# Low parts of weights made by GpSimd in the first mixer, and its chunks placed on consecutive groups

## The chip, the cores and the metric

The kernel runs on one core of one Trainium2 chip. The metric is device time in microseconds of the whole kernel, lower is better. Times come from repeated runs and from one execution that the hardware profiler recorded. Engines are named as in the profile: PE (TensorE), DVE (VectorE), ACT (ScalarE), POOL (GpSimd), SP (SyncE, which here only issues transfers).

## The reference

Two layers of a decoder trunk on x of 256 tokens by 2048 features, all in float32. Each layer has a mixer and an MLP, both modulated by a condition vector c:

```python
cond = silu(c)
for l in range(2):
    sh1, sc1, g1, sh2, sc2, g2 = split(cond @ w_mod[l] + b_mod[l], 6)      # w_mod[l]: 2048 x 12288
    u = x * (1 + sc1) + sh1
    q, k, v, gate_b, gate_c, h_in = split(u @ w_in[l])                     # w_in[l]: 2048 x 6144
    attn = dilated_mixture(rotary(q), rotary(k), v)                        # 8 heads of 128
    conv = gate_b * causal_short_conv(gate_c * h_in, conv_w[l])
    mixed = group_rms_norm(concat(attn, conv), mix_norm_g[l])
    x = layer_norm(alpha * x + (1 + g1) * (mixed @ w_out[l]), ...)         # w_out[l]: 2048 x 2048
    u = x * (1 + sc2) + sh2
    ff = square(relu(u @ w_ff1[l])) @ w_ff2[l]                             # 2048 x 8192, 8192 x 2048
    x = layer_norm(alpha * x + (1 + g2) * ff, ...)
```

## The kernel before, in words

**Units, groups, labels.** Every large product is cut into units of 512 output columns, and a unit into 8 groups (`GROUPS`) of two 128-row blocks of the weights. One group of weights is 128 partitions by 1024 elements (`GW`), 512 KB. A label numbers the groups through the whole kernel: label = 8 * unit + j. The first mixer has 16 units (12 of `w_in`, 4 of `w_out`), labels 0 to 127. The first three units (labels 0 to 23, `START_GROUPS`) are done in another way, at the start, while the modulation for them is computed. The MLP of the layer follows with 64 units, then the second layer.

**High and low parts.** To keep float32 accuracy, weights and activations are split in a high part, as PE reads it, and the remainder, the low part. For each label from 24 on:
- SP loads the weights into `raw[:, j % 4]` (four slots, line 426). It waits until the low part of the label four before has been made, since that is the last reader of the slot.
- ACT copies them to `w_hi[:, j % 4]` (line 516, semaphore `hi_ready`). It waits for the transfer and for PE to have done the group four before.
- DVE subtracts, `w_lo = raw - w_hi` (line 836, semaphore `lo_ready`, counted in order of labels).
- PE waits for `lo_ready` and does 12 matmuls of 512 columns: for two row blocks and two token tiles, high by high, low by high, high by low (lines 1367 to 1369; in halves of one token tile lines 1381 to 1383).

ACT and DVE run `ahead`: at position p (the turn of label p) they prepare label p + 4, then do what `side` asks for at p.

**The last unit.** In the last unit of a mixer or MLP, groups 4 to 7 are done for the first token tile and then again for the second. DVE's `last_tile` (from line 1012) finishes the first tile, gives it its normalisation while PE does the second tile, and the fill of the next unit (transposes of the normalised x, line 1513) starts from there. GpSimd normalises two of the four quarters of each tile (line 483, a tensor-scalar on 128 x 512), DVE one (line 969), ACT one.

**Chunks.** The modulation is a product of c with `w_mod`, too long and thin for PE; DVE does it beside the rest, one chunk of 128 x 1024 elements (512 KB) at a time: line 858 for slabs used as columns (a multiplication by `cond_row` with a sum), lines 846 and 850 for slabs used as gates. 16 chunks make a slab. GpSimd's loop issues the chunk transfers (line 496) into four slots of `mod_raw`; each waits until DVE has done the chunk four before (`mod_used`). The list `MOD_AT`, from `mod_positions`, says at which positions DVE does a chunk: in the first mixer 96 chunks (6 slabs), at every position from 25 to 71, and from 72 to 126 at all but those with p % 8 = 7. `side` of DVE does the chunk first and then whatever else stands at p. At p % 8 = 7 of units 12 to 14 that is `residual`, which waits for the unit's last group. After the last slab that `modulation` of the next fill needs, its columns are summed.

**Order.** Each engine runs its own list, in order, and waits on counting semaphores. GpSimd's list is: chunk issues in a hardware loop of four per turn, `normalise` at each fill, and again.

Of the kernel before, what the change touches and what calls it, by code (L numbers as in the profile page):

```python
# [28 lines left out]
F32 = mybir.dt.float32  # L29
# [49 lines left out]
def mod_positions():  # L79

    mixer0 = [p for p in range(START_GROUPS + 1, 8 * U_MIX) if p % 8 != 7 or p < 72]
    ff0 = sorted([8 * w + j for w in range(2, FF_UNITS - 1) for j in (1, 3, 4, 6)]
                 + [8 * w + 7 for w in (2, 3, 8, 9, 10, 11, 16, 17, 18, 19, 24, 25)])
    mixer1 = sorted([8 * u + j for u in range(2, 15) for j in (0, 2, 4, 6)]
                    + [8 * u + 1 for u in range(2, 14)])
    ff1 = sorted([8 * w + 4 for w in range(3, 25)] + [8 * w + 1 for w in range(3, 13)])
    out = []
    for base, count, local in ((MIXER_AT[0], MIX_SLABS[0], mixer0), (FF_AT[0], FF_SLABS[0], ff0),
                               (MIXER_AT[1], MIX_SLABS[1], mixer1), (FF_AT[1], FF_SLABS[1], ff1)):
        assert len(local) == count * KC  # L90
        out += [base + p for p in local]
    return out
# [67 lines left out]
MIX_GAIN_AT = (9, 11, 13, 17)  # L160
FF_GAIN_AT = (8 + 1, 8 + 4, 8 + 6, 16 + 1)


# [43 lines left out]
def build(nc, x, cond_c, ln_cols, w_in, w_out, w_ff1, w_ff2, w_mod, b_mod, b_rows, conv_w, mix_g, ln1_g, ln1_b,  # L207
# [3 lines left out]
    with ctx:  # L211
# [90 lines left out]
        hi_ready = sem("hi_ready")  # L302
        lo_ready = sem("lo_ready")
        pair_used = sem("pair_used")
        mod_used = sem("mod_used")
# [81 lines left out]
        def prepared(unit, j):  # L387

            return 8 * unit + (j + 1 - START_GROUPS)

        def wait_job(eng, n):

# [3 lines left out]
        def _(sp):  # L396
# [22 lines left out]
            def load(weights, row, unit, j, from_head=False):  # L419
                slot = j % RAW  # L420
                if from_head and j < START_LABELS:
                    sp.wait_ge(pair_used, START_GROUPS - 2 * START_LABELS + j + 1)
                elif not from_head or j >= RAW:

                    sp.wait_ge(lo_ready, prepared(unit, j - RAW))
                sp.dma_start(raw[:, slot:slot + 1, :],
                             weights[bass.ds(row, 1), :, :].rearrange("a p n -> p a n")).then_inc(raw_in[slot], 16)

            for layer in range(DEPTH):
                base = U_LAYER * layer  # L430
                if layer == 0:
# [6 lines left out]
                    for j in range(GROUPS):  # L438
                        load(w_in, START_GROUPS + j, START_UNITS, j, from_head=True)
                first = START_UNITS + 1 if layer == 0 else 0  # L440
                with sp.Fori(first, U_IN) as u:
                    for j in range(GROUPS):
                        load(w_in, (u + layer * U_IN) * GROUPS + j, u + base, j)
                with sp.Fori(0, U_OUT) as u:
                    for j in range(GROUPS):
                        load(w_out, (u + layer * U_OUT) * GROUPS + j, u + (base + U_IN), j)
                with sp.Fori(0, BLOCKS) as b:
# [13 lines left out]
        def _(pool):  # L461
# [23 lines left out]

            ends, q = [], 0
            for count in (MIX_SLABS[0], FF_SLABS[0], MIX_SLABS[1]):
                q += count * KC
                ends.append(q // MODS + 1)
            ends.append((SLABS - START_SLABS) * KC // MODS)  # L490
            start = 1
            for i, end in enumerate(ends):
                with pool.Fori(start, end) as r:
                    for k in range(MODS):
                        pool.wait_ge(mod_used, MODS * r + (first + k - MODS + 1))
                        pool.dma_start(mod_raw[:, k:k + 1, :], chunk(r * MODS + (first + k))).then_inc(mod_in[k], 16)  # L496
                if i < 3:
                    normalise(i + 1)
# [326 lines left out]
        def _(dve):  # L825
# [7 lines left out]

            def prepare(unit, j):
                dve.wait_ge(hi_ready, prepared(unit, j))
                nc.vector.tensor_tensor(weights(w_lo, u_lo, unit, j), raw[:, j % RAW, :],  # L836
# [512 lines left out]
        def _(pe):  # L1349
# [6 lines left out]
            def group(label, slot, k0, acc_pair, hi, lo):  # L1356


                pe.wait_ge(lo_ready, label + 1 - START_GROUPS)
                for kk in range(GK):  # L1360
# [11 lines left out]
            def half(unit, j, o, t, hi, lo):  # L1372


                pe.wait_ge(lo_ready, prepared(unit, j))
                for kk in range(GK):
# [348 lines left out]
```

## Time and profile before

| what | value |
|---|---|
| runs | 2330.39, 2333.58, 7494.66 us; median 2333.58 |
| profiled execution | 2329.62 us |
| its span | 2327.9 us |
| TensorE busy | 2253.6 us (97%) |
| DVE busy | 1707.9 us (73%) |
| ACT busy | 1079.8 us (46%) |
| GpSimd busy | 227.6 us (10%) |
| mean granted TensorE clock | 0.989 of 2.4 GHz |
| transfers | 623.10 MB, 268 GB/s over the span |

The span is the time between the first and the last instruction in the profile; the execution's own time is a little longer. Busy times are sums of instruction durations, and issuing a transfer counts as GpSimd's only where a row shows it. "Landing" is the time from the issue of a transfer until its data are there. Matmuls overlap: one is shown as 0.39 us, but the next starts 0.23 us after it.

### The profile page before, as it was taken

To read this page: it belongs to the slowest core of one execution; us is meant where nothing else is said; L and a number is where in the kernel's file an instruction comes from. 1 tells how busy PE (TensorE), PEld (TensorE's weight loads), DVE (VectorE), ACT (ScalarE), POOL (GpSimd) and SP (SyncE) were. 2 spreads that over 40 slices of the span, in tenths; PEclk is the share of its full clock that TensorE was granted. 3 is DMA by queue.
4 is the path that set the end of the run, shared out by engine and by line. 5 is a ranking of instruction groups with operands and counts; after the bars stand their busy time and mean duration, and the time that the engine had idled before them with its cause. 6 is when DMAs were issued, how large, how long until landed. Compare 5 with 4: busy or idle time off the path is not lost.

```text
span 2327.9 us, 29649 instructions
## 1 busy us (share of the span) xinstructions
PE 2253.6 (97%) x10064; PEld 1824.3 (78%) x10064; DVE 1707.9 (73%) x2200; ACT 1079.8 (46%) x1372; POOL 227.6 (10%) x400
## 2 busy tenths in 40 slices
PE   6899999989999999999999999999999999999997
PEld 3368887768888888888878888877888888888886
DVE  5799988977777777778878878877665555555566
ACT  1146543366345445445454564436644543543542
POOL 2301111111001011011010111101000000000000
PEclk8999999989999999999999999999999999999999
DMA  9988998958888888888866788886677676666574
GB/s 378 409 328 303 337 343 296 362 189 277 280 293 303 277 300 302 289 293 289 315 216 219 259 271 287 297 303 204 194 235 248 223 227 217 210 203 197 173 228 134
DMA packets 174731, 623.10 MB, mean 268 GB/s; under 512 B 19728, under 2 KB 20496, under 8 KB 174096
## 3 DMA queue, kind: packets, MB, share of 16 engines
q1 hardware_dynamic: 114128, 407.50, 50.8%
q0 software_dynamic: 55296, 201.35, 25.5%
q10 hardware_dynamic: 5184, 12.59, 1.7%
q8 instruction: 80, 1.31, 0.2%
q14 instruction: 43, 0.35, 0.0%
HBM read 619.27 MB, written 2.10 MB: 267 GB/s over the span
## 4 chain that ended last, share of the span: by engine, by line
PE 84%; DVE 7%; DMA 6%; issue 2%; ACT 1%; ACTq 1%; POOLq 0%; DVEq 0%; SPq 0%; POOL 0%
PE bank L1367 26%; PE bank L1369 26%; PE bank L1368 26%; DMA Z<-w_mod_dram 4%; PE bank L1460 2%; DVE w_lo L836 2%; DMA raw<-w_out_dram 1%; DVE mod_raw L858 1%; PE bank L1381 1%; PE bank L1383 1%; PE bank L1382 1%; DVE Z L858 1%; ACT w_hi L516 1%; ACTq L588 1%; PE bank L1446 1%
## 5 line engine op out<-in xcount | busy, mean ns | idle before, releaser
L836 DVE TENSOR_TENSOR w_lo<-raw,w_hi 128x1024 fp32r<-128x1024 f32 x740 | 903.4, 1224 | 517.4 <-ACT w_hi L516 515.5
L516 ACT ACTIVATE w_hi<-raw 128x1024 fp32r<-128x1024 f32 x740 | 782.1, 1059 | 1020.5 <-PE bank L1369 915.1
L1367 PE MATMUL bank<-w_hi,u_hi 128*128 128x512 f32 x1648 | 652.8, 396 | 0.0
L1369 PE MATMUL bank<-w_lo,u_hi 128*128 128x512 f32 x1648 | 642.1, 390 | 0.0
L1368 PE MATMUL bank<-w_hi,u_lo 128*128 128x512 f32 x1648 | 641.8, 389 | 0.0
L1367 PE MATMUL bank<-w_hi,m_hi 128*128 128x512 f32 x1200 | 470.1, 392 | 4.4 <-DVE m_lo L906 2.5
L1369 PE MATMUL bank<-w_lo,m_hi 128*128 128x512 f32 x1200 | 467.8, 390 | 0.0
L1368 PE MATMUL bank<-w_hi,m_lo 128*128 128x512 f32 x1200 | 467.6, 390 | 0.0
L1369 PEld LDWEIGHTS bank<-w_lo,u_hi 128*128 128x128 f32 x1648 | 309.3, 188 | 65.3
L1367 PEld LDWEIGHTS bank<-w_hi,u_hi 128*128 128x128 f32 x1648 | 309.5, 188 | 63.9 <-issue 1.2
L1368 PEld LDWEIGHTS bank<-w_hi,u_lo 128*128 128x128 f32 x1648 | 309.7, 188 | 63.5 <-issue 1.2
L496 POOL DMA_DIRECT2D mod_raw<-w_mod_dram x316 | 167.3, 529 | 1709.3 <-DVE mod_raw L858 756.7
L1367 PEld LDWEIGHTS bank<-w_hi,m_hi 128*128 128x128 f32 x1200 | 225.7, 188 | 52.9 <-DVE m_lo L906 3.3
L1368 PEld LDWEIGHTS bank<-w_hi,m_lo 128*128 128x128 f32 x1200 | 225.7, 188 | 47.0 <-issue 0.5
L1369 PEld LDWEIGHTS bank<-w_lo,m_hi 128*128 128x128 f32 x1200 | 225.5, 188 | 47.1
L858 DVE SCALAR_TENSOR_TENSOR mod_raw<-mod_raw,cond_row 128x1024 f32<-128x1024 f32 x192 | 234.0, 1219 | 4.1 <-DMA mod_raw<-w_mod_dram 4.0
L850 DVE SCALAR_TENSOR_TENSOR mod_acc<-mod_raw,cond,mod_acc 128x1024 f32<-128x1024 f32 x120 | 153.5, 1279 | 0.0
L858 DVE SCALAR_TENSOR_TENSOR Z<-Z,cond_row 128x1024 f32<-128x1024 f32 x64 | 77.3, 1223 | 34.4 <-DMA Z<-w_mod_dram 31.0
L1497 PE MATMUL bank<-raw,utmp 128*128 128x512 f32 x96 | 48.5, 657 | 19.4 <-DMA raw<-w_in_dram 11.0
L906 DVE TENSOR_TENSOR m_lo<-utmp,m_hi 128x512 fp32r<-128x512 f32 x72 | 49.2, 692 | 13.0 <-ACT m_hi L540 12.9
L1460 PE MATMUL bank<-idn,Z 128*128 128x128 f32 x416 | 54.1, 273 | 2.5 <-DVE Z L1207 1.4
L1460 PEld LDWEIGHTS bank<-idn,Z 128*128 128x128 f32 x416 | 48.4, 141 | 9.6 <-DVE Z L1207 1.8
(151 smaller groups left out, 1257.2 us busy)
## 6 DMA issues: line engine op xcount, KB each, us to landing
raw<-w_ff_dram SPq DMA_DIRECT2D x512, 512.0 KB, 4.0
mod_raw<-w_mod_dram POOLq DMA_DIRECT2D x320, 512.0 KB, 5.2
raw<-w_in_dram SPq DMA_DIRECT2D x180, 512.0 KB, 5.3
Z<-w_mod_dram POOLq DMA_DIRECT2D x64, 512.0 KB, 12.5
raw<-w_out_dram SPq DMA_DIRECT2D x64, 512.0 KB, 5.9
gate<-w_in_dram SPq DMA_DIRECT2D x8, 512.0 KB, 8.9
gate<-b_rows_dram ACTq DMA_DIRECT2D x4, 1024.0 KB, 4.9
Z<-ln_g_dram ACTq DMA_DIRECT2D x16, 256.0 KB, 6.3
```

Of the source, the lines that this page charges most:

```text
L496: pool.dma_start(mod_raw[:, k:k + 1, :], chunk(r * MODS + (first + k))).then_inc(mod_in[k], 16)
L516: nc.scalar.activation(weights(w_hi, u_hi, unit, j), raw[:, j % RAW, :], ACT.Copy).then_inc(hi_ready, 1)
L588: act.dma_start(lngb[:, s, a, :], src[layer:layer + 1, s * NCOL:(s + 1) * NCOL] .to_broadcast([P, NCOL])).then_inc(gb_in[s], 16)
L836: nc.vector.tensor_tensor(weights(w_lo, u_lo, unit, j), raw[:, j % RAW, :], weights(w_hi, u_hi, unit, j).bitcast(F32), ALU.subtract).then_ ...
L850: ins = nc.vector.scalar_tensor_tensor(out=mod_acc[:], in0=src, scalar=cond[:, k:k + 1], in1=mod_acc[:], op0=ALU.mult, op1=ALU.add)
L858: nc.vector.scalar_tensor_tensor(out=src, in0=src, scalar=1.0, in1=cond_row[:, half], op0=ALU.mult, op1=ALU.mult, accum_out=mod_part[:, i: ...
L906: nc.vector.tensor_tensor(lo[:, chunk:chunk + 2, :], src, hi[:, chunk:chunk + 2, :].bitcast(F32), ALU.subtract).then_inc(split_ready, 1)
L1367: nc.tensor.matmul(o, hi[:, k, tok], wh, start=(k == 0), stop=False)
L1368: nc.tensor.matmul(o, lo[:, k, tok], wh, start=False, stop=False)
L1369: ins = nc.tensor.matmul(o, hi[:, k, tok], wl, start=False, stop=(k == KC - 1))
L1460: ins = nc.tensor.transpose(b[:, c * SEQ + t * P:c * SEQ + (t + 1) * P], src(c, t), idn[:])
L1497: ins = nc.tensor.matmul(start_acc[unit][t][:], utmp[:, e % 2, tok], place[:, c * NCOL:(c + 1) * NCOL], start=(s == 0), stop=(s == KC - 1))
```

## The change

It has two parts, both in the first mixer alone.

1. The 96 chunks are done at positions 24 to 119, one at each. The last unit (positions 120 to 127) has none.
2. For labels 31, 35, ..., 119 (23 of them, all in slot 3) GpSimd makes the low part. The instruction stands in GpSimd's loop behind the four chunk issues of a turn and waits for the high part of label 4r + 27. DVE skips these labels. Whoever waited for the low part of a label (PE, and SP for the raw slot) now waits for `pool_lo` on these labels, and on the others for `lo_ready` with the count reduced by GpSimd's. So that the counts are constants, SP's two hardware loops over the units of the first mixer are written out.

The start of GpSimd's loops moves by one turn for the first stage's end, so that turn r always meets label 4r + 27.

```diff
--- before.py
+++ after.py
@@ -78,7 +78,7 @@
 
 def mod_positions():
 
-    mixer0 = [p for p in range(START_GROUPS + 1, 8 * U_MIX) if p % 8 != 7 or p < 72]
+    mixer0 = list(range(START_GROUPS, START_GROUPS + MIX_SLABS[0] * KC))
     ff0 = sorted([8 * w + j for w in range(2, FF_UNITS - 1) for j in (1, 3, 4, 6)]
                  + [8 * w + 7 for w in (2, 3, 8, 9, 10, 11, 16, 17, 18, 19, 24, 25)])
     mixer1 = sorted([8 * u + j for u in range(2, 15) for j in (0, 2, 4, 6)]
@@ -159,6 +159,19 @@
 GAIN_ORDER = {1: (0, 1, 2, 3), 2: (2, 0, 1, 3), 3: (0, 1, 2, 3)}
 MIX_GAIN_AT = (9, 11, 13, 17)
 FF_GAIN_AT = (8 + 1, 8 + 4, 8 + 6, 16 + 1)
+
+
+POOL_FIRST, POOL_LAST = START_GROUPS + 2 * AHEAD - 1, START_GROUPS + MIX_SLABS[0] * KC - 1
+
+
+def on_pool(label):
+
+    return label % AHEAD == AHEAD - 1 and POOL_FIRST <= label <= POOL_LAST
+
+
+def pool_count(label):
+
+    return max(0, (min(label, POOL_LAST) - POOL_FIRST) // AHEAD + 1)
 
 def start_order(p):
@@ -301,6 +314,7 @@
         gb_in = [sem(f"gb_in{j}") for j in range(4)]
         hi_ready = sem("hi_ready")
         lo_ready = sem("lo_ready")
+        pool_lo = sem("pool_lo")
         pair_used = sem("pair_used")
         mod_used = sem("mod_used")
         cond_exp = sem("cond_exp")
@@ -388,6 +402,13 @@
 
             return 8 * unit + (j + 1 - START_GROUPS)
 
+        def wait_low(eng, label):
+
+            if on_pool(label):
+                eng.wait_ge(pool_lo, pool_count(label))
+            else:
+                eng.wait_ge(lo_ready, label + 1 - START_GROUPS - pool_count(label))
+
         def wait_job(eng, n):
 
             eng.wait_ge(t_done, n + 1)
@@ -420,9 +441,12 @@
                 slot = j % RAW
                 if from_head and j < START_LABELS:
                     sp.wait_ge(pair_used, START_GROUPS - 2 * START_LABELS + j + 1)
-                elif not from_head or j >= RAW:
-
-                    sp.wait_ge(lo_ready, prepared(unit, j - RAW))
+                elif isinstance(unit, int):
+                    if not from_head or j >= RAW:
+                        wait_low(sp, GROUPS * unit + j - RAW)
+                else:
+
+                    sp.wait_ge(lo_ready, prepared(unit, j - RAW) - pool_count(POOL_LAST))
                 sp.dma_start(raw[:, slot:slot + 1, :],
                              weights[bass.ds(row, 1), :, :].rearrange("a p n -> p a n")).then_inc(raw_in[slot], 16)
 
@@ -437,13 +461,19 @@
                     sp.wait_ge(mod_used, START_SLABS * KC - 4)
                     for j in range(GROUPS):
                         load(w_in, START_GROUPS + j, START_UNITS, j, from_head=True)
-                first = START_UNITS + 1 if layer == 0 else 0
-                with sp.Fori(first, U_IN) as u:
-                    for j in range(GROUPS):
-                        load(w_in, (u + layer * U_IN) * GROUPS + j, u + base, j)
-                with sp.Fori(0, U_OUT) as u:
-                    for j in range(GROUPS):
-                        load(w_out, (u + layer * U_OUT) * GROUPS + j, u + (base + U_IN), j)
+                    for u in range(START_UNITS + 1, U_MIX):
+                        for j in range(GROUPS):
+                            if u < U_IN:
+                                load(w_in, u * GROUPS + j, u, j)
+                            else:
+                                load(w_out, (u - U_IN) * GROUPS + j, u, j)
+                else:
+                    with sp.Fori(0, U_IN) as u:
+                        for j in range(GROUPS):
+                            load(w_in, (u + layer * U_IN) * GROUPS + j, u + base, j)
+                    with sp.Fori(0, U_OUT) as u:
+                        for j in range(GROUPS):
+                            load(w_out, (u + layer * U_OUT) * GROUPS + j, u + (base + U_IN), j)
                 with sp.Fori(0, BLOCKS) as b:
                     for half, weights in enumerate((w_ff1, w_ff2)):
                         for u in range(4):
@@ -484,9 +514,10 @@
                                                 ALU.add).then_inc(xhat_pool, 1)
 
             ends, q = [], 0
+            assert START_GROUPS + AHEAD * (MIX_SLABS[0] * KC // MODS) - 1 == POOL_LAST
             for count in (MIX_SLABS[0], FF_SLABS[0], MIX_SLABS[1]):
                 q += count * KC
-                ends.append(q // MODS + 1)
+                ends.append(q // MODS + (1 if ends else 0))
             ends.append((SLABS - START_SLABS) * KC // MODS)
             start = 1
             for i, end in enumerate(ends):
@@ -494,6 +525,11 @@
                     for k in range(MODS):
                         pool.wait_ge(mod_used, MODS * r + (first + k - MODS + 1))
                         pool.dma_start(mod_raw[:, k:k + 1, :], chunk(r * MODS + (first + k))).then_inc(mod_in[k], 16)
+                    if i == 0:
+
+                        pool.wait_ge(hi_ready, AHEAD * r + AHEAD)
+                        nc.gpsimd.tensor_tensor(w_lo[:, AHEAD - 1, :], raw[:, RAW - 1, :], w_hi[:, AHEAD - 1, :].bitcast(F32),
+                                                ALU.subtract).then_inc(pool_lo, 1)
                 if i < 3:
                     normalise(i + 1)
                 start = end
@@ -832,6 +868,8 @@
                 dve.wait_ge(dve_step, step[0])
 
             def prepare(unit, j):
+                if on_pool(GROUPS * unit + j):
+                    return
                 dve.wait_ge(hi_ready, prepared(unit, j))
                 nc.vector.tensor_tensor(weights(w_lo, u_lo, unit, j), raw[:, j % RAW, :],
                                         weights(w_hi, u_hi, unit, j).bitcast(F32), ALU.subtract).then_inc(lo_ready, 1)
@@ -1356,7 +1394,7 @@
             def group(label, slot, k0, acc_pair, hi, lo):
 
-                pe.wait_ge(lo_ready, label + 1 - START_GROUPS)
+                wait_low(pe, label)
                 for kk in range(GK):
                     k = k0 + kk
                     wh = w_hi[:, slot, kk * NCOL:(kk + 1) * NCOL]
@@ -1372,7 +1410,7 @@
             def half(unit, j, o, t, hi, lo):
 
-                pe.wait_ge(lo_ready, prepared(unit, j))
+                wait_low(pe, GROUPS * unit + j)
                 for kk in range(GK):
                     k = GK * j + kk
                     wh = weights(w_hi, u_hi, unit, j)[:, kk * NCOL:(kk + 1) * NCOL]
```

## Rows read from the trace of the kernel before

Timelines give start, duration, engine, line, instruction, and in brackets the idle time before it and who ended it. Groups give count, busy us, mean ns, and the idle time before them. In the table of stretches the engines are in the order PE, PEld, DVE, ACT, POOL, each with its count of instructions in brackets.

**Rows 1.** Chain that ended last, whole span: shares by engine.

```profile
PE 84%; DVE 7%; DMA 6%; issue 2%; ACT 1%; ACTq 1%; POOLq 0%; DVEq 0%; SPq 0%; POOL 0%
```

**Rows 2.** Stretches: length, busy us of each engine, granted clock, DMA share, GB/s.

```profile
133.49:450.67 317.18, 309.95 (x1459) 255.57 (x1457) 289.15 (x429) 148.50 (x228) 47.05 (x89) 0.99 0.90 323
450.67:464.22 13.55, 11.94 (x49) 8.59 (x47) 10.04 (x16) 2.99 (x3) 3.17 (x6) 1.00 0.95 337
464.22:492.53 28.31, 18.61 (x81) 14.64 (x81) 22.37 (x48) 18.83 (x36) 8.60 (x5) 0.76 0.55 183
1579.85:1590.74 10.89, 10.89 (x49) 8.96 (x48) 6.09 (x17) 4.51 (x6) 1.15 (x1) 1.00 0.47 171
1590.74:1610.39 19.65, 15.47 (x81) 12.03 (x80) 15.96 (x30) 16.48 (x33) 6.92 (x4) 1.00 0.56 191
```

**Rows 3.** Timeline of PE: start, duration, instruction, idle before it.

```profile
428.73 0.50 PE L1367 MATMUL bank<-w_hi,m_hi 128*128 128x512 f32 x1 [0.70 <-DVE w_lo L836]
470.63 0.69 PE L1513 MATMUL bank<-idn,xt 128*128 128x128 f32 x2 [6.41 <-ACT xt L599]
492.53 0.40 PE L1367 MATMUL bank<-w_hi,u_hi 128*128 128x512 f32 x1
1610.39 0.40 PE L1367 MATMUL bank<-w_hi,u_hi 128*128 128x512 f32 x1
```

**Rows 4.** Timeline of DVE at the ends of the first and second mixer.

```profile
464.19 1.22 DVE L858 SCALAR_TENSOR_TENSOR mod_raw<-mod_raw,cond_row 128x1024 f32<-128x1024 f32 x1 [1.32 <-DMA mod_raw<-w_mod_dram]
465.75 0.69 DVE L1012 TENSOR_TENSOR bank<-bank,gate 128x512 f32<-128x512 f32 x1
1585.49 0.70 DVE L1012 TENSOR_TENSOR bank<-bank,gate 128x512 f32<-128x512 f32 x1 [3.06 <-PE bank L1383]
```

**Rows 5.** Groups of DVE, 124 to 466 us: count, busy us, mean ns, idle before.

```profile
L836 DVE TENSOR_TENSOR w_lo<-raw,w_hi 128x1024 fp32r<-128x1024 f32 x104 | 126.8, 1222 | 26.2 <-ACT w_hi L516 25.7
L858 DVE SCALAR_TENSOR_TENSOR mod_raw<-mod_raw,cond_row 128x1024 f32<-128x1024 f32 x64 | 78.0, 1219 | 4.1 <-DMA mod_raw<-w_mod_dram 4.0
```

**Rows 6.** The high parts among ACT's groups, 124 to 466 us.

```profile
L516 ACT ACTIVATE w_hi<-raw 128x1024 fp32r<-128x1024 f32 x105 | 110.5, 1058 | 141.3 <-PE bank L1369 94.3 <-DMA raw<-w_out_dram 29.1 <-PE bank L1383 6.7
```

**Rows 7.** Groups of POOL, whole span.

```profile
L496 POOL DMA_DIRECT2D mod_raw<-w_mod_dram x316 | 167.3, 529 | 1709.3 <-DVE mod_raw L858 756.7 <-DVE mod_acc L850 690.8 <-DVE mod_acc L846 243.7
```

**Rows 8.** GpSimd's line 483: duration ns min/median/max; all twelve, then one alone.

```profile
L483 POOL TENSOR_SCALAR xt<-xt,rst,nmu x12: 762/2040/3256, 469.8 to 1598.5; 128x512 f32<-128x512 f32 x12
L483 POOL TENSOR_SCALAR xt<-xt,rst,nmu x1: 3256/3256/3256, 475.6 to 475.6; 128x512 f32<-128x512 f32 x1
```

**Rows 9.** Timeline of DVE beside that one GpSimd instruction and the next.

```profile
477.18 1.22 DVE L836 TENSOR_TENSOR w_lo<-raw,w_hi 128x1024 fp32r<-128x1024 f32 x1
478.31 0.85 DVE L969 TENSOR_SCALAR xt<-xt,rst,nmu 128x512 f32<-128x512 f32 x1
479.08 1.21 DVE L836 TENSOR_TENSOR w_lo<-raw,w_hi 128x1024 fp32r<-128x1024 f32 x1
```

**Rows 10.** Line 969 of DVE: duration ns min/median/max.

```profile
L969 DVE TENSOR_SCALAR xt<-xt,rst,nmu x6: 547/694/847, 469.8 to 1598.0; 128x512 f32<-128x512 f32 x6
```

**Rows 11.** Waits of SP's DMA queue, 140 to 466 us: total us, times, longest.

```profile
SPq L426 <- DVE w_lo L836: 255.1, 101, 7.0
```

**Rows 12.** Median issue to landing, us: chunks 320 to 380, weights 400 to 440.

```profile
mod_raw<-w_mod_dram POOLq DMA_DIRECT2D x18, 512.0 KB, 6.3
raw<-w_out_dram SPq DMA_DIRECT2D x13, 512.0 KB, 7.6
```

**Rows 13.** Timelines of DVE and PE around labels 87 and 111.

```profile
332.45 1.23 DVE L836 TENSOR_TENSOR w_lo<-raw,w_hi 128x1024 fp32r<-128x1024 f32 x1 [0.35 <-ACT w_hi L516]
339.25 0.39 PE L1367 MATMUL bank<-w_hi,u_hi 128*128 128x512 f32 x1
412.00 1.22 DVE L858 SCALAR_TENSOR_TENSOR mod_raw<-mod_raw,cond_row 128x1024 f32<-128x1024 f32 x1
414.27 0.39 PE L1367 MATMUL bank<-w_hi,m_hi 128*128 128x512 f32 x1
```

## The prediction, made before the result was known

> **What bounds the kernel now.** I read the chain of waits first, to learn whose time is worth anything. TensorE holds 84% of it, VectorE (DVE) 7%, transfers 6% [rows 1]. So a change to DVE's load pays only in the few places where TensorE stands still.
>
> The second view is a table of stretches, laid over the first mixer. There the labels 24 to 123 take 317.18 us, and TensorE is busy for 309.95 of them: 7.2 us idle in 100 groups, although DVE is busy for 289.15 us, or 91% [rows 2]. The granted clock is 0.99. A group takes 3.17 us on average with the work between groups, four groups 12.7 us. Where there is no work between them it is 2.72 us, four of them 10.9 us: the second mixer's last unit does the work of four groups in 10.89 us [rows 2].
>
> What follows is different. The last unit's eight half groups take 13.55 us, and the fill from there to the fifth group of the MLP takes 28.31 us. The second mixer ends in the same instructions, and there the two take 10.89 and 19.65 us. The timeline says why: TensorE idles for 6.41 us before its first transpose at 470.63 [rows 3], because DVE is still on chunks. The chunk of position 126 runs at 464.19, having waited for its transfer, and only then does DVE start line 1012 on the first token half, at 465.75. In the second mixer line 1012 waited for TensorE, not TensorE for it [rows 4]. After the 6.41 us without matmuls the granted clock of the fill is 0.76, so part of it ran at 1.2 GHz in place of 2.4; at the second mixer's end it stays 1.00 [rows 2].
>
> **The change, part by part.** The sum is made against the profiled execution, 2329.62 us (span 2327.9 and 1.7 around it). The three runs have a median 4.0 us above it, the lowest 0.8 above.
>
> *Chunks on every position from 24 to 119.* Seven chunks leave the last unit (120 to 126) and fill the skipped positions 79, 87, 95, 103, 111, 119 and 24. With DVE free of them, line 1012 can start when TensorE's first half is done, as at 1585.49 [rows 4]. I price this by the second mixer's end: the halves 13.55 - 10.89 = 2.7 us, the fill 28.31 - 19.65 = 8.7 us, clock included [rows 2]. The stall of 0.70 us before label 116, which waited for a low half [rows 3], goes too. **Gain 12.1 us.** What is late next there is TensorE's own end of the second token half, as in the second mixer.
>
> *DVE's load.* 23 low parts of 1.22 us leave it [rows 5], 28 us in all. Most of that was slack: label 87's low part started at 332.45 and ended 5.6 us before its group at 339.25 [rows 13]. So I count nothing for it beyond the 0.70 above. The cover is TensorE's own 2.7 us a group.
>
> *GpSimd's instruction.* No tensor-tensor of GpSimd is in the trace. The nearest is its tensor-scalar on 512 elements with one input, 0.76 us at the shortest and 3.26 at the longest [rows 8]. Twice the elements give 1.5 us, twice the inputs as well 3.0; twice the longest is 6.5. I take **2.3 us**, the middle of the undisturbed pair, and keep 1.5 and 6.5 for the range. The Trainium skill (GPSIMD Engine Reference, Elementwise side-by-side cycle accounting) measures 4497 ns for such an addition on 2048 elements, from which I estimate about 2.2 us by proportion, and the sum would be the same; the trace has no row for it.
>
> Why 3.26 happens is visible. That instruction ran from 475.6 while DVE went from one instruction with two SBUF inputs to the next, and it got done only around line 969 at 478.31 [rows 8, 9]. So GpSimd can be kept out by DVE. In turn line 969 took 0.85 us there against 0.55 at best [rows 9, 10]: DVE is kept out too, by 0.3 us at least.
>
> *Where it lies in GpSimd's queue.* The subtraction stands behind the four chunk issues of its turn of the loop, and the fourth waits until DVE has done the chunk of position 23 + 4r. Label 87 shows a normal cycle: DVE began its low part at 332.45, when the high part came. Without it DVE does the chunk there, until 333.7, and has a gap until the next high part. GpSimd issues the transfer (0.53 us [rows 7]) and subtracts until about 336.5, 2.7 us before group 87 at 339.25 [rows 13]. So no stall. The chunk issues of the next turn stand behind the subtraction, but their first slot comes free only after DVE's next low part and chunk, 2.4 us of work, so they lose nothing.
>
> *Raw slot 3.* Its next load now waits for GpSimd and starts some 2.8 us later, and the loads of slots 0 to 2 stand behind it in SP's queue, which waited 255.1 us in 101 waits for low parts [rows 11] and so has room. The slot's round is landing + 1.06 (high part [rows 6]) + 0.5 + 2.3. At 6.3 us landing that is 10.2 us, under 10.9 and 12.7. Around labels 107 to 119 weights take 7.6 us [rows 12], and the round is 11.5. There I follow the cycle: chunk 107 would be done at 412.0, where it starts now, GpSimd ends at 412.0 + 0.5 + 2.3 = 414.8, and group 111 starts at 414.27 [rows 13]: 0.5 us late. Label 115 is loaded 2.8 us later than now, and its own low part ends 1.6 later after that (2.3 + 0.5 for 1.2): 4.4 against 2.3 us that label 111 has to spare now and I take for 115 too, and 0.5 of it is already paid: 1.6 us more. With two more chunks of 0.52 MB in a stretch whose transfers are 0.95 busy at 337 GB/s [rows 2], 1.6 us each and half of it in the open, **the cost is 4 us**.
>
> *The rest.* SP's loop written out removes branches from a queue that waits anyway: nothing. Reductions of gate slabs move by one position: nothing.
>
> Sum: 2329.6 - 12.1 + 4 = **2321.5**, and with half of the 4.0 us between profile and median, **2323 us**.
>
> **Rivals.** *The slot's round becomes the bound (slower).* If GpSimd's subtraction takes 6.5 us because DVE, 91% busy, keeps it out, the round is 6.3 + 1.06 + 0.5 + 6.5 = 14.4 us against 12.7: 1.7 us in each of 23 rounds, 39 us, less the 12: 2357. It decides from 4.8 us, where the round meets 12.7; at that price only the ten rounds or so without work in between pay, 1.8 each, 18 us, and the time is 2336. For it: the 3.26 us row. Against it: DVE has a gap exactly where the low part was taken out, and idles 26 us waiting for high parts in this stretch [rows 5]. Chance 0.20.
>
> *GpSimd does not relieve DVE.* Each subtraction holds the second DVE instruction out for its 2.3 us while it saves 1.22. I allow eight of the 23 to fall where DVE has a backlog; there it comes 1.1 us further back each time, 9 us; with the other 4 the gain is spent: about 2331. For it: line 969's 0.3 us. Against it: DVE's low parts at 477.18 and 479.08, beside GpSimd's work, took their usual 1.22 and 1.21 [rows 9]. The Trainium skill (SBUF — State Buffer, Who interferes with whom) states this rule: a DVE instruction with two SBUF inputs and a GpSimd instruction that reads SBUF exclude each other for the whole instruction, whoever comes first. The trace agrees on both sides, with the two delays above, and by it alone the time would be the 2331 of this case. Chance 0.18.
>
> *More than forecast.* All 7.2 us idle in the groups goes as well and slot 3 costs nothing: 2329.6 - 12.1 - 7.2 = 2310. It needs all of that idle to hang on DVE. Chance 0.05.
>
> The forecast itself has 0.57: its own range is 2317 (no cost) to 2329.
>
> **The numbers.** Below 2316 lies half of the third rival, above 2345 the worse half of the first: the range is 2316 to 2345. A difference of 2% is 47 us, which is also about what a measurement of this kernel tells from no change. No case gains it: 12.1 + 7.2 is under 20 us. The slot's round would have to cost 59, beyond 6.5 us per subtraction. So faster 0.02, within 2% 0.93, slower 0.05.
>
> **What would show it.** In the profile after: no chunk on DVE behind about 450 us before the fill, the wait of 6.41 us before the first transpose gone, the fill near 20 us with the clock at about 1.0, the halves near 11. GpSimd's new group of 23 instructions at about 2.3 us mean; a mean over 3.5 speaks for the first rival, and TensorE would then wait for w_lo out of GpSimd, every fourth group. DVE's low or chunk steps longer than 1.3 us beside GpSimd's would show the exclusion; with the fill short and the groups longer by 9 us that is the second rival. I am wrong altogether if DVE still comes late to line 1012, for instance because chunks land late.

## The result, and the profile after

The changed kernel is slower: 2353.12 us median (2350.37 to 2354.99) against 2333.58, ratio 1.0088 with a 95% interval of 1.0075 to 1.0102. Ratios, here and below, leave out runs more than 1.5% above the fastest of their kernel, such as the one of 7494.66 us, so they can differ a little from quotients of the medians. The profiled execution took 2350.37 us, its span 2348.7, against 2329.62 and 2327.9. I had forecast 2323 us, in a range of 2316 to 2345.

The table of stretches of the kernel after, cut at the same instructions as [rows 2] (labels 24 to 123; the last unit's half groups; the fill to the fifth group of the MLP). Columns: length, busy us of PE, PEld, DVE, ACT, POOL, granted clock, DMA share, GB/s.

```profile
133.82:484.09 350.27, 322.01 (x1457) 262.03 (x1456) 309.49 (x422) 150.82 (x229) 105.55 (x115) 0.96 0.85 297
484.09:495.11 11.02, 11.02 (x48) 9.07 (x49) 8.22 (x18) 3.45 (x5) 1.14 (x1) 1.00 0.55 192
495.11:514.74 19.63, 15.45 (x82) 12.04 (x80) 15.95 (x30) 16.47 (x33) 9.05 (x8) 1.00 0.80 293
```

The end of the mixer came out as forecast. The halves take 11.02 us in place of 13.55 and the fill 19.63 in place of 28.31, with the clock at 1.00: 11.2 us gained. The 6.41 us before the first transpose are gone (no idle time stands before it), and DVE's line 1012, now 1050, waits for TensorE again:

```profile
495.11 1.03 PE L1551 MATMUL bank<-idn,xt 128*128 128x128 f32 x8
```

```profile
489.86 0.70 DVE L1050 TENSOR_TENSOR bank<-bank,gate 128x512 f32<-128x512 f32 x1 [2.42 <-PE bank L1421]
```

But labels 24 to 123 take 350.27 us where they took 317.18: 33.1 us lost. Of these 21.0 are idle time of TensorE (28.3 against 7.2), and 12.1 are matmuls that took longer (322.01 busy against 309.95), because the granted clock fell to 0.96 from 0.99. It falls behind the long waits. The same view shows it for two shorter stretches, the first with a wait of 3.75 us in it, the second without any:

```profile
173.00:190.00 17.00, 12.12 (x52) 9.65 (x51) 15.21 (x19) 6.19 (x18) 5.12 (x6) 0.80 0.79 253
330.00:385.00 55.00, 55.00 (x257) 45.89 (x256) 50.85 (x67) 23.75 (x26) 21.91 (x23) 1.00 0.91 328
```

What TensorE waited for between 130 and 490 us (line waiting, who ended the wait, total us, times, longest):

```profile
PE bank L1484 <- DVE Z L1181: 5.9, 1, 5.9
PE bank L1578 <- DVE Z L1255: 4.9, 3, 3.8
PE bank L1635 <- ACT Z L771: 4.5, 1, 4.5
PE bank L1405 <- POOL w_lo L531: 3.4, 3, 2.0
PE bank L1498 <- DVE gate L939: 2.4, 1, 2.4
```

Only 3.4 us are GpSimd's low parts coming late. The rest are steps of attention, convolution and reduction that DVE, or ACT behind DVE, finished late. DVE lost 23 low parts and is still busy for 309.49 us, more than the 289.15 before. (Seven more chunk steps stand in this stretch now; with them and all low parts, but without GpSimd's subtractions, it is 297.08, as a kernel below shows.) Its groups, and GpSimd's new instruction (count, busy us, mean ns, idle before):

```profile
L874 DVE TENSOR_TENSOR w_lo<-raw,w_hi 128x1024 fp32r<-128x1024 f32 x80 | 113.3, 1419 | 36.8 <-ACT w_hi L552 36.5
L896 DVE SCALAR_TENSOR_TENSOR mod_raw<-mod_raw,cond_row 128x1024 f32<-128x1024 f32 x64 | 87.3, 1377 | 1.3 <-DMA mod_raw<-w_mod_dram 1.3
L1273 DVE SCALAR_TENSOR_TENSOR Z<-Z,cw 128x256 f32<-128x256 f32 x16 | 11.5, 778 | 0.1
L1260 DVE TENSOR_SCALAR nmx<-mx 128x2 f32<-128x2 f32 x8 | 6.0, 749 | 0.3
```

```profile
L531 POOL TENSOR_TENSOR w_lo<-raw,w_hi 128x1024 fp32r<-128x1024 f32 x23 | 55.8, 2424 | 2.2
```

The low parts take 1419 ns on average in place of 1222, the column chunks 1377 in place of 1219 [rows 5]. GpSimd's subtraction takes 2.42 us, near the 2.3 that I took. Its 23 instructions can be laid beside DVE's in the two timelines. Beside 20 of them a DVE instruction takes over 0.15 us more than the shortest of its kind, in sum 39.7 us more, 2.0 us each, where 23 low parts of 1.22 us save 28. Beside the other three DVE was idle, or did instructions that read no more than one input from SBUF.

### The profile page after: what moved, and what is told of

Read it like the earlier page. It is cut to its first block, busy times and chain, and to the rows that moved or that the text cites. A ratio compares the mean times of both kernels' runs of the same rounds, so it can differ in the third digit from the quotient of the medians.

```text
span 2348.7 us, 29404 instructions
## 1 busy us (share of the span) xinstructions
PE 2259.9 (96%) x10064; PEld 1827.4 (78%) x10064; DVE 1719.8 (73%) x2177; ACT 1080.3 (46%) x1372; POOL 284.8 (12%) x423
## 4 chain that ended last, share of the span: by engine, by line
PE 80%; DVE 10%; DMA 6%; issue 2%; ACT 1%; ACTq 1%; POOL 0%; POOLq 0%; DVEq 0%; SPq 0%
PE bank L1405 24%; PE bank L1407 24%; PE bank L1406 24%; DMA Z<-w_mod_dram 4%; DVE w_lo L874 2%; PE bank L1498 2%; DVE mod_raw L896 2%; DVE mod_acc L888 1%; DMA raw<-w_out_dram 1%; PE bank L1419 1%; PE bank L1421 1%; PE bank L1420 1%; ACT w_hi L552 1%; PE bank L1484 1%; DMA mod_raw<-w_mod_dram 1%
## 5 line engine op out<-in xcount | busy, mean ns | idle before, releaser
L874 DVE TENSOR_TENSOR w_lo<-raw,w_hi 128x1024 fp32r<-128x1024 f32 x717 | 891.0, 1246 | 527.4 <-ACT w_hi L552 525.7
L896 DVE SCALAR_TENSOR_TENSOR mod_raw<-mod_raw,cond_row 128x1024 f32<-128x1024 f32 x192 | 243.2, 1271 | 1.3 <-DMA mod_raw<-w_mod_dram 1.3
L1535 PEld LDWEIGHTS bank<-raw,utmp 128*128 128x128 f32 x96 | 19.7, 215 | 49.9 <-issue 40.3
```

What stands on the lines that cost most here:

```text
L896: nc.vector.scalar_tensor_tensor(out=src, in0=src, scalar=1.0, in1=cond_row[:, half], op0=ALU.mult, op1=ALU.mult, accum_out=mod_part[:, i: ...
L1535: ins = nc.tensor.matmul(start_acc[unit][t][:], utmp[:, e % 2, tok], place[:, c * NCOL:(c + 1) * NCOL], start=(s == 0), stop=(s == KC - 1))
```

## The experiments

Unless a line says otherwise, times are medians of the whole kernel. "Behind" is how much later TensorE starts a label in the profiled execution of one kernel than in that of another. "The reductions" are those of the two gate slabs that fall in the first mixer. Two theories came first: that GpSimd and DVE exclude each other, one standing still while the other works (1), and that the chunks' new places make DVE late (2). A third was the raw slot's longer round (3). Theory 2 later splits in two: the moved reductions (2a) or the seven added chunk steps (2b). The diffs show the lines that matter, against the changed kernel; `...` stands for what is left out of a line.

### Chunks moved, no low part by GpSimd

```diff
-    return label % AHEAD == AHEAD - 1 and POOL_FIRST <= label <= POOL_LAST
+    return False
-                        nc.gpsimd.tensor_tensor(w_lo[:, AHEAD - 1, :], raw[:, RAW - 1, :], ...)
```

> The chunks stand at 24 to 119 as in the changed kernel, and DVE makes every low part; GpSimd makes none. Theory 1 (exclusion: GpSimd's subtraction and DVE's two-input instructions keep each other out, DVE gets late with attention and convolution steps, TensorE loses 32 us before label 123): that loss goes and the gain at the end of the first mixer stays, 11 us: about 2322 us, label 123 within 3 us of the kernel before. Theory 2 (placement: seven more chunks before label 120 make DVE late): most of the 32 us stays, 2345 us or more. Theory 3 (the slot's round, raw slot 3 freed late): as theory 1, about 2322.

Measured: 2334.0 us, ratio 1.0003 (0.9994 to 1.0013). Neither theory had this number. Label 123 starts 12.7 us behind the kernel before, and the mixer's end gives 9.8 of it back. So the subtractions cost 19 us, and the moved chunks as they stood bring nothing. TensorE's waits in this kernel name two places:

```profile
204.54 0.42 PE L1493 MATMUL bank<-idn,Z 128*128 128x128 f32 x1 [2.60 <-DVE gate L934]
305.71 0.70 PE L1479 MATMUL bank<-mod_acc,ones 128*128 128x512 f32 x1 [3.25 <-DVE Z L1176]
```

Line 934 is DVE's reading of a reduced gate slab. The positions of these reductions are worked out from the chunk list, two behind a slab's last chunk and past positions that are taken. With the list one earlier they fell from 43 and 74 to 41 and 73. At 41 the reduction now stands ahead of the transposes of k at 42, which need its bank; at 73 it meets DVE one group sooner, still at the convolution's product.

### The same with the reductions back, and the whole change with them back

```diff
-RED_NOT_BEFORE = {16: MIXER_AT[1] + 8, 17: MIXER_AT[1] + 12}
+RED_NOT_BEFORE = {4: 43, 5: 74, 16: MIXER_AT[1] + 8, 17: MIXER_AT[1] + 12}
```

> The kernel with the chunks moved only (DVE makes every low part), and the two reductions of gate slabs, which follow the chunk list and so had moved from positions 43 and 74 to 41 and 73, put back to 43 and 74. Theory 2a (the reductions: at 41 the transposes of k at 42 wait behind them for DVE's reading of the bank, 2.6 us, and at 73 TensorE waits 3.25 us for DVE): label 123 comes from 12.7 us behind the kernel before to 4 to 6 behind, and the whole is 2325 to 2328 us, faster than before. Theory 2b (seven more chunk steps on DVE): unchanged, 2334 us.

> The changed kernel with GpSimd's subtractions, and the two reductions back at 43 and 74. Theory 1 and 2a together: the exclusion's part stays, 17 to 20 us over the kernel with chunks moved and reductions back: 2343 to 2347 us. If the two only add where they meet (DVE late at these reductions because of the exclusion), more comes back: 2338.

Measured: without subtractions 2325.13 us, ratio 0.9968 (0.9957 to 0.9979), faster than both kernels; label 123 is 3.7 us behind. The moved reductions thus cost about 8 us, and theory 2a holds. With subtractions 2346.57, ratio 1.0062 (1.0045 to 1.0079): the reductions cost 6.5 us there, and the subtractions 21 on top of the better kernel. The three stretches in the kernel with 2325.13; its fill is 7.9 us shorter than before, and its labels 24 to 123 take 4.9 us more:

```profile
133.60:455.64 322.04, 311.66 (x1458) 256.78 (x1457) 297.08 (x445) 150.31 (x229) 48.58 (x92) 0.99 0.90 324
455.64:466.60 10.96, 10.96 (x48) 9.07 (x49) 8.14 (x18) 3.40 (x6) 1.06 (x1) 1.00 0.55 194
466.60:487.00 20.40, 16.62 (x83) 13.09 (x81) 16.05 (x30) 16.54 (x33) 9.10 (x8) 0.92 0.81 287
```

### Nobody makes the 23 low parts

TensorE and the raw slot wait for the high part instead; this part of the computation is left out.

```diff
-                        nc.gpsimd.tensor_tensor(w_lo[:, AHEAD - 1, :], raw[:, RAW - 1, :], ...)
-                eng.wait_ge(pool_lo, pool_count(label))
+                eng.wait_ge(hi_ready, label + 1 - START_GROUPS)
```

> The changed kernel with GpSimd's 23 subtractions left out and nobody making those low parts (that part of the computation is missing); TensorE and the raw slot wait for the high part instead. DVE keeps the relief, and there is no exclusion. Theory 1: the loss before label 123 goes and some of the 7 us that TensorE idled there before goes too: 2314 to 2321 us. Theory 2: 2340 or more. Theory 3: 2314 to 2321, and DVE's low parts as long as before in theories 1 and 3 both (1.22 us).

> The 23 low parts made by nobody (that part is missing), chunks at 24 to 119, reductions at 43 and 74: what DVE's relief would be worth for nothing. Against the kernel with reductions back (2325.1): theory 1 says the relief is worth little once DVE is not late at the reductions, 3 to 5 us: 2320 to 2322. If the relief is worth what it was with the reductions moved (11.6 us): 2313 to 2315.

Measured: 2322.39 us (0.9958, 0.9944 to 0.9972) with the reductions moved, 2321.33 (0.9949, 0.9937 to 0.9962) with them back. The first is just above the 2314 to 2321 that theory 1 gave: TensorE still loses time at the moved reductions. DVE's low parts are back at their old length:

```profile
L869 DVE TENSOR_TENSOR w_lo<-raw,w_hi 128x1024 fp32r<-128x1024 f32 x89 | 108.5, 1223 | 39.6 <-ACT w_hi L547 39.1
```

So DVE's relief, had it been free, is worth 11.6 us where the reductions stand badly, but only 4 us where they stand well (0.9949 against 0.9968). And what the subtractions do to the others costs 31 us gross in the changed kernel (2353.1 against 2322.4), the waits for GpSimd's own low parts among it.

### A subtraction that nobody needs, and memsets

```diff
+                pool.wait_ge(hi_ready, AHEAD * r + AHEAD)
+                nc.gpsimd.tensor_tensor(m_lo[:, 12:16, :], cond_row[:, 0:GW]..., cond_row[:, GW:2 * GW]...,
+                                        ALU.subtract).then_inc(pool_lo, 1)
```

or, in its place, three times

```diff
+                    nc.gpsimd.memset(m_lo[:, 12:16, :].bitcast(F32), 0.0).then_inc(pool_lo, 1)
```

The target is free until position 100, so there are 17 turns of it; DVE waits once, at that position, for the last. DVE makes all low parts in both.

> The kernel with the chunks moved only, and in the first 17 turns GpSimd also does a subtraction of 1024 elements that nobody needs, from two SBUF inputs of its own, behind the same high part. No low part, no slot and no TensorE wait hangs on it. Theory 1: DVE's instructions get longer beside it and, since DVE has no relief, label 96 starts at least as late as in the changed kernel, 23 us behind the kernel before, perhaps 35; the whole 2345 to 2360 us. Theory 3 and theory 2: as the kernel with the chunks moved only, within 3 us.

> As the one before, but in place of the subtraction three memsets of 1024 elements, that write and read nothing. GpSimd's queue is held for a similar time (an estimate: 2 to 3 us a turn). Theory 1 (exclusion by reads): DVE's low parts stay at 1.22 us and the time is that of the chunks moved only, within 3 us. If instead the time in GpSimd's queue, behind which the next chunk transfers are issued, makes the loss: as the subtraction, 2345 us or more.

Measured: the subtraction 2357.15 us, ratio 1.0105 (1.0088 to 1.0122), 23 us over the kernel without it, though no low part, slot or matmul waits for it. The memsets 2336.95, ratio 1.0020 (1.0010 to 1.0029): 3 us by the medians and 4 by the ratios, at the edge of what I allowed or just over it. In GpSimd's time the two are alike:

```profile
L530 POOL TENSOR_TENSOR m_lo<-cond_row 128x1024 fp32r<-128x1024 f32 x17 | 45.8, 2693 | 0.4
```

```profile
L530 POOL MEMSET m_lo<- 128x1024 f32 x51 | 49.6, 972 | 2.0
```

In DVE's they are not. First the kernel with the subtraction, then the one with memsets (low parts, column chunks, and a tensor-scalar of the convolution with one SBUF input):

```profile
L880 DVE TENSOR_TENSOR w_lo<-raw,w_hi 128x1024 fp32r<-128x1024 f32 x102 | 130.0, 1276 | 19.8 <-ACT w_hi L558 19.4
L902 DVE SCALAR_TENSOR_TENSOR mod_raw<-mod_raw,cond_row 128x1024 f32<-128x1024 f32 x64 | 91.4, 1429 | 1.3 <-DMA mod_raw<-w_mod_dram 1.1
```

```profile
L878 DVE TENSOR_TENSOR w_lo<-raw,w_hi 128x1024 fp32r<-128x1024 f32 x108 | 131.7, 1222 | 28.5 <-ACT w_hi L556 28.1
L1277 DVE TENSOR_SCALAR Z<-Z,cw 128x256 f32<-128x256 f32 x8 | 6.1, 828 | 0.0
```

Memsets leave the two-input instructions alone and lengthen the tensor-scalar (350 ns in the kernel before, 828 here). A GpSimd instruction that reads lengthens both; this tensor-scalar takes 677 ns on average in the kernel with the useless subtraction. Theory 3 falls as the cause of the 19 us, and so does the time in GpSimd's queue: the cost is there with nobody waiting for GpSimd, and mostly gone when GpSimd is as long busy without reading. The Trainium skill (SBUF — State Buffer, Who interferes with whom) states that GpSimd and DVE exclude each other where GpSimd reads and DVE takes two inputs from SBUF, and not where GpSimd only writes; both kernels here agree, with 1276 and 1222 ns for the low part.

### Subtractions with the old chunk places

```diff
-    mixer0 = list(range(START_GROUPS, START_GROUPS + MIX_SLABS[0] * KC))
+    mixer0 = [p for p in range(START_GROUPS + 1, 8 * U_MIX) if p % 8 != 7 or p < 72]
```

> GpSimd makes the same 23 low parts, at the same labels, but the chunks and reductions stand where they stood before the change; GpSimd's list of the first mixer is written out, each subtraction at the place in it where it has the same wait. Theory 1: the exclusion costs some 17 us before label 123 and the last unit and the fill stay long: 2345 to 2355 us. If the placement of chunks is what makes the exclusion cost: within 4 us of the kernel before.

Measured: 2348.19 us, ratio 1.0070 (1.0054 to 1.0087). The subtractions alone, on the kernel before, cost 15 us (16 by the ratio), and the end of the mixer stays long. On the two kernels with moved chunks they cost 19 and 21. So the two parts of the change are nearly independent: their costs add up to within about 5 us.

### Other places for the chunks

```diff
-    mixer0 = list(range(START_GROUPS, START_GROUPS + MIX_SLABS[0] * KC))
+    mixer0 = [p for p in range(START_GROUPS + 1, 123) if p not in (111, 119)]
```

and `[p for p in range(START_GROUPS + 1, 122) if p != 95]`, both with the reductions back and no subtraction.

> No low part by GpSimd; reductions at 43 and 74; the 96 chunks at 25 to 122 without 111 and 119, so that position 24 and two turns with a residual step have none and the last unit has three. The gain at the end of the mixer should stay, since line 1012 starts when TensorE's first half is done, about position 124: 2322 to 2326 us by theory 2a; by 2b, with four of the seven chunks still moved, 2328.

> No low part by GpSimd, reductions at 43 and 74, the 96 chunks at 25 to 121 without 95. The turns around the second convolution and normalisation (95) and the first (24) have none, two stand in the last unit. Theory 2a, by what the kernel with reductions back still loses (0.6 us at label 36, 2.9 us at labels 99 and 100): 2322 to 2324 us. If those two losses are not due to the chunks at 24 and 95: 2325.

Measured: 2324.74 us (0.9969, 0.9959 to 0.9978) and 2326.72 (0.9978, 0.9968 to 0.9988). The first is as expected, the second misses its 2322 to 2325. It has no loss at labels 99 and 100 any more, but starts 3.0 us later at 116 and 117, so label 123 is 2.4 us behind in place of 3.7, and the halves of its last unit, with two chunks in it, take 12.5 us. Nothing is gained over chunks at 24 to 119.

### Where the exclusion costs

Theory 1 in its full form says that a subtraction costs nothing where no step of DVE that TensorE waits for is made late. Against it stood a plain share of 21.4 / 23 = 0.9 us each, wherever it is, and theory 4, that lateness must add up over turns in a row.

With reductions back and chunks at 24 to 119, GpSimd makes fewer low parts. Its list of the first mixer is written out for this.

```diff
-    return label % AHEAD == AHEAD - 1 and POOL_FIRST <= label <= POOL_LAST
+    return label in POOL_LABELS
```

> The kernel with reductions back, and GpSimd makes 4 low parts only, labels 79, 83, 87 and 91, where DVE has no attention or convolution step and low parts are ready 5.6 us before their groups. Theory 1 in its full form (the exclusion costs time only where a step of DVE that TensorE waits for is made late): DVE's instructions get longer there too, and the time stays, 2325 us within 1.5. If each subtraction costs its share (21.4 / 23 = 0.9 us): 2329.

> The same with 4 low parts by GpSimd at labels 39, 43, 71 and 95, made beside attention steps, the second rotation and the two convolutions. Theory 1: 4 to 9 us over the kernel with reductions back: 2329 to 2334 us, TensorE losing at labels 42 to 47, 72 and 96 to 100. If each costs its share: 2329; if there is no difference of place, the same as the run with labels 79 to 91.

> The kernel with reductions back and 12 low parts by GpSimd, every eighth label from 31 to 119, so that a turn without one follows each. Theory 4 (lateness adds up: one subtraction costs DVE's list about 1 us net, which the slack of two or three groups takes up, and only one in every turn in a row outruns it): under 4 us over the kernel with reductions back, 2325 to 2329 us. Theory 1 in its share form (0.9 us each): 11 us, 2336.

> Eight low parts by GpSimd in a row of turns, labels 31 to 59 (the attention heads of the first four and the second rotation). Theory 4: as in the kernel with all 23 up to there, TensorE 7 us behind at label 51 against the kernel with reductions back, and nothing after: 2331 to 2334 us. The share form: 8 x 0.9 = 7 us too, but spread over the turns. If it needs the backlog of later steps: 2326.

> Ten low parts in a row of turns, labels 63 to 99 (both convolutions and normalisations with a quiet stretch between). Theory 4: 5 to 8 us over the kernel with reductions back, lost at labels 71 to 75 and 96 to 99 and nothing between 76 and 95: 2330 to 2333 us. The share form: 9 us, spread.

Measured, with TensorE's lateness against the kernel with reductions back (start of a label's first matmul, set to zero at label 30), in us:

| labels by GpSimd | us | ratio | at 39 | 55 | 76 | 95 | 102 | 123 |
|---|---|---|---|---|---|---|---|---|
| 79, 83, 87, 91 | 2327.46 | 0.9982 (0.9973 to 0.9991) | -0.1 | -0.1 | -0.1 | -0.1 | 0.7 | 1.1 |
| 39, 43, 71, 95 | 2328.51 | 0.9982 (0.9973 to 0.9991) | -0.1 | -0.1 | 0.5 | 0.5 | 1.1 | 1.1 |
| 31 to 59 (8) | 2329.91 | 0.9992 (0.9983 to 1.0001) | 4.8 | 5.7 | 5.7 | 5.7 | 4.1 | 6.7 |
| 63 to 99 (10) | 2335.03 | 1.0016 (1.0007 to 1.0025) | -0.1 | -0.1 | 3.5 | 3.5 | 7.3 | 7.7 |
| every eighth (12) | 2335.49 | 1.0011 (1.0002 to 1.0020) | 2.7 | 3.4 | 4.8 | 4.8 | 6.9 | 10.1 |
| all (23) | 2346.57 | 1.0062 (1.0045 to 1.0079) | 4.3 | 6.5 | 12.3 | 12.8 | 16.4 | 20.6 |

In every one of them TensorE loses nothing between labels 76 and 95, or almost: the subtractions there cost no time where they run, and four of these kernels have three or more of them there. The loss comes at 36 and 37, 47 to 51, 71 to 75, 96 to 99, and 111 to 119. So by the traces the place matters. The times of the whole kernels do not show it: 2327.46 misses the 2325 within 1.5 of the full form, and by the ratios the quiet four and the busy four both cost 3.3 us over the kernel with reductions back (0.9982 against 0.9968), 0.8 us each. The intervals of these ratios overlap, so 3.3 us is hardly told from nothing, or from the 1.1 us of the traces. My "busy" labels, forecast at 2329 or more, missed most of the places that lose.

Each row is one execution, and that sets a limit. The kernel with labels 31 to 59 loses 2.6 us at labels 116 to 118, where none of its subtractions is left, and wins 1.5 at 99 and 100. A step of 1 or 2 us in one row proves nothing; what stands is what several rows have at the same place.

Theory 4 falls: with a free turn after each, twelve subtractions still cost 10 us, where it allowed under 4. By the ratios the rows with eight or more cost 0.7 to 1.1 us for each subtraction.

The kernel with the quiet four shows the exclusion itself. GpSimd, and then DVE, in the timeline around 337 us:

```profile
336.54 2.41 POOL L531 TENSOR_TENSOR w_lo<-raw,w_hi 128x1024 fp32r<-128x1024 f32 x1
```

```profile
337.13 2.92 DVE L887 TENSOR_TENSOR w_lo<-raw,w_hi 128x1024 fp32r<-128x1024 f32 x1 [1.43 <-ACT w_hi L565]
339.96 1.21 DVE L909 SCALAR_TENSOR_TENSOR mod_raw<-mod_raw,cond_row 128x1024 f32<-128x1024 f32 x1
```

DVE's low part begins at 337.13, while GpSimd is at work, and takes 2.92 us in place of 1.22. It ends 1.1 us after GpSimd's end at 338.95 (336.54 + 2.41), which is about its usual time: it was held until GpSimd had finished. GpSimd was not longer for it. Here DVE had slack, and no matmul was late.

## Why the prediction was wrong

- **The end of the mixer** (gain 11.4 by the stretches, 12.1 with the stall before label 116): right. 11.2 us came in the two stretches, by the steps described, clock included. The stall is gone in the changed kernel, but not because of the chunks: with reductions back and no subtraction TensorE still waits 0.97 us before label 116.
- **"Reductions of gate slabs move by one position: nothing"**: wrong, and it failed twice. They moved by two and one (43 to 41, 74 to 73), and the first thereby passed the transposes of k. This cost 8 us with DVE making all low parts. I had read the list of chunk positions and not what is computed from it.
- **GpSimd's instruction, 2.3 us**: right, 2.42.
- **What it does to DVE**: the step that failed most. The sum has no term for it: the subtraction was to run in a gap of DVE and hold nobody, and it cost 19 us net, 15 on the old chunk places, 21 on the good ones. I had the rule, as the second rival with 2331 us, and allowed eight of 23 subtractions to cost 1.1 us each, 9 us; in the trace 20 of 23 held a DVE instruction, for 39.7 us in all. The sign that the prediction named for it, low or chunk steps over 1.3 us, is there with 1419 and 1377 ns. I argued against the rival with [rows 9], where DVE's low parts kept their 1.22 us beside GpSimd's work. Those were cases in which DVE had begun first or GpSimd's instruction had only just been issued. They say nothing of a DVE instruction that begins while GpSimd is reading. Nor was line 969, which I took for the rule, a case of it: it has one SBUF input. It belongs with the tensor-scalars that memsets lengthened. The "gap where the low part was taken out", my argument for an undisturbed subtraction, served GpSimd, which was never held for long (2.35 to 2.81 us), and let DVE's next instruction run into it.
- **The clock**: missing from the price of waits. 12.1 of the 33.1 us lost are matmuls at the lower level behind waits of 2 to 6 us. I had seen this at the fill and counted it there, not in the rivals. The size varies: with reductions back and all subtractions, matmuls of the same labels took 6.1 us longer (316.09 against 309.95 busy), also behind waits of up to 4.5 us.
- **DVE's relief counted as nothing**: 4 us with the reductions well placed, so nearly right; 11.6 with them moved.
- **Raw slot 3, 4 us**: of the right size. TensorE waited 3.4 us for GpSimd's low parts: 1.96 at label 111 and 0.65 at 119, in the stretch that I had priced, and 0.80 at 71, which I had not. No run takes the slot's round apart from GpSimd's lateness by being held behind chunk issues.
- **Seven more chunk steps before label 120**, counted only as transfers: label 123 comes 3.7 us later in the kernel with the reductions back, mainly at 99 and 100. TensorE waits there 2.0 us in place of 0.9 for ACT, at the sums of squares behind the second convolution.
- **The first rival** (the slot's round, slower): right in sign, wrong in mechanism.

The sum, by ratios against about 2333 us: chunks moved -7.5, reductions moved +8.2, subtractions +19.8, together +20.5. My 2323 us is close to what the chunks alone give with the reductions in place, 2325, but in part by luck: it holds 4 us for slot 3, which that kernel does not pay, and leaves out the 4.9 us that labels 24 to 123 lose there.

Open in part is why labels 36 and 37 lose time. They lose 4 to 5 us in the kernels where GpSimd makes 31 and 35, 2.6 where it makes 31 and 39 (every eighth), and nothing where it makes 39 and 43. So each of 31 and 35 seems to bring about half; 39 brings none. In the changed kernel the subtraction for 31 held a chunk step 1.6 us, and the one for 35 held the small tensor-scalar of the attention step 2.3 us. The wait that ends there is TensorE's on the scores' mask step, which stands behind both in DVE's list. I ran no kernel that moves one subtraction by one turn.

## What to carry to other kernels

Work moved to GpSimd that reads SBUF is paid by DVE for as long as it has a two-input instruction ready beside it: here up to 2.7 us held, 2.0 on average in the 20 cases, for 1.2 us saved. It can pay only if DVE has at that moment slack that nobody waits for, and no kernel here gained by it; look for the steps in DVE's list that TensorE or ACT wait on, not at DVE's busy share. When a list of positions is changed, print what is derived from it, before and after.

## What the runs showed of the hardware

- The tensor-scalar on 128 x 2 elements of the attention step took 0.17 us alone, 0.60 beside a memset of GpSimd (until 165.46 us) and 2.50 beside a subtraction of GpSimd (166.05 to 168.44 us): even the smallest instruction is held. First two of the kernel with memsets, then one of the changed kernel:

```profile
158.86 0.17 DVE L1266 TENSOR_SCALAR nmx<-mx 128x2 f32<-128x2 f32 x1
164.89 0.60 DVE L1266 TENSOR_SCALAR nmx<-mx 128x2 f32<-128x2 f32 x1
```

```profile
165.97 2.50 DVE L1260 TENSOR_SCALAR nmx<-mx 128x2 f32<-128x2 f32 x1
```

- A DVE instruction whose record began just before GpSimd's was held too, in the changed kernel; GpSimd's row stands first, then DVE's. The chunk step began 0.22 us earlier by the records, took 3.67 us in place of 1.22, and GpSimd's was no longer than usual:

```profile
313.77 2.35 POOL L531 TENSOR_TENSOR w_lo<-raw,w_hi 128x1024 fp32r<-128x1024 f32 x1
```

```profile
313.55 3.67 DVE L896 SCALAR_TENSOR_TENSOR mod_raw<-mod_raw,cond_row 128x1024 f32<-128x1024 f32 x1
```

- Instructions of DVE with one input in PSUM and one in SBUF were not lengthened, nor were the statistics, with one input in SBUF. Beside the subtraction of 426.96 to 429.37 us in the changed kernel they took 0.68 to 0.69 us each, as on average in the kernel before (684 and 686 ns). Each line shows two of them, which overlap by some 0.08 us:

```profile
427.33 1.28 DVE L1121 SCALAR_TENSOR_TENSOR xt<-xt,bank 128x512 f32<-128x512 f32 x2
428.64 1.29 DVE L1126 BATCH_NORM_STATS2 stats<-xt 128x6 f32<-128x512 f32 x2
```
